# Two more weight tiles of each next matrix split ahead of a matrix boundary, in the idle activation region

## The reference

```python
h = rmsnorm(x, norm1_g[i]) * (1.0 + scale1) + shift1
y = diff_attention(h, ...)                 # i == 0: a_w_qkv, a_w_o
x = x + gate1 * y
h = rmsnorm(x, norm2_g[i]) * (1.0 + scale2) + shift2
x = x + gate2 * swiglu(h, f_w_in[i], f_w_out[i])
...
h2 = rms_norm(x, ffn_norm_g[layer])
up = h2 @ w_up[layer]
x = x + (jax.nn.gelu(conv(a)) * val) @ w_down[layer]
```

## Time and profile before

| | us |
|---|---|
| median of 3 runs (1039.02 to 1041.01) | 1040.88 |
| span of the profiled execution, first to last instruction | 1033.8 |
| PE busy | 986.3 |
| VectorE busy | 740.2 |
| ScalarE busy | 542.6 |

### The profile page before, as it was taken

The page is one execution under the profiler, slowest core; times in us unless marked ns, Lnnn a source line. Parts: engine busy times, 40 slices in busy tenths (PEclk is TensorE's granted clock), DMA queues, the critical chain, the costliest instruction groups (busy, mean ns, idle before and its releaser), DMA issues.

```text
span 1033.8 us, 13550 instructions
## 1 busy us (share of the span) xinstructions
PE 986.3 (95%) x5102; PEld 827.2 (80%) x5102; DVE 740.2 (72%) x1053; ACT 542.6 (52%) x875; POOL 68.4 (7%) x126
## 2 busy tenths in 40 slices
PE   2999799999999999999999999999999999999997
PEld 2887577888878787778888886888888779999986
DVE  5988888878877897887665447647753777777643
ACT  4466846544443485575444436575546474444442
POOL 2100222000000411010000002000000010000000
PEclk8999999999999999999999999999999999999999
DMA  9998167998889472449865553856444367656551
GB/s 339 371 371 285 39 204 230 344 321 295 273 304 359 162 250 101 143 127 321 263 203 186 183 184 108 269 160 205 134 142 143 119 190 218 187 177 189 184 184 41
DMA packets 126968, 219.89 MB, mean 213 GB/s; under 512 B 9235, under 2 KB 78088, under 8 KB 126904
## 3 DMA queue, kind: packets, MB, share of 16 engines
q1 hardware_dynamic: 125200, 215.52, 63.4%
q0 software_dynamic: 1088, 2.87, 0.8%
q10 hardware_dynamic: 616, 0.65, 0.2%
HBM read 217.96 MB, written 1.05 MB: 212 GB/s over the span
## 4 chain that ended last, share of the span: by engine, by line
PE 84%; DVE 8%; ACT 4%; issue 2%; DMA 1%; POOL 0%; SPq 0%; POOLq 0%; DVEq 0%; ACTq 0%
PE bank L1900 13%; PE bank L1902 13%; PE bank L1901 13%; PE bank L1913 5%; PE bank L1915 5%; PE bank L1914 5%; PE bank L2504 3%; PE bank L2505 3%; PE bank L2506 3%; DVE w_lo L1156 2%; PE bank L1961 2%; PE bank L1963 2%; PE bank L1962 2%; ACT w_hi L638 1%; DVE ada_acc L1186 1%
## 5 line engine op out<-in xcount | busy, mean ns | idle before, releaser
L1156 DVE TENSOR_TENSOR w_lo<-raw,w_hi 128x1024 fp32r<-128x1024 f32 x312 | 379.1, 1223 | 215.3 <-ACT w_hi L638 214.5
L638 ACT ACTIVATE w_hi<-raw 128x1024 fp32r<-128x1024 f32 x312 | 328.2, 1061 | 338.4 <-PE bank L1902 139.7
L1900 PE MATMUL bank<-w_hi,h_hi 128*128 128x512 f32 x608 | 244.3, 402 | 3.7 <-DVE w_lo L1156 3.7
L1902 PE MATMUL bank<-w_hi,h_lo 128*128 128x512 f32 x608 | 238.3, 392 | 0.0
L1901 PE MATMUL bank<-w_lo,h_hi 128*128 128x512 f32 x608 | 237.9, 391 | 0.0
L1900 PEld LDWEIGHTS bank<-w_hi,h_hi 128*128 128x128 f32 x608 | 114.8, 189 | 28.4 <-issue 6.1
L1902 PEld LDWEIGHTS bank<-w_hi,h_lo 128*128 128x128 f32 x608 | 114.7, 189 | 24.6
L1901 PEld LDWEIGHTS bank<-w_lo,h_hi 128*128 128x128 f32 x608 | 114.9, 189 | 23.6 <-issue 1.0
L2504 PE MATMUL bank<-h_hi,w_hi 128*128 128x256 f32 x320 | 90.8, 284 | 1.1 <-DVE conv_t L1828 1.1
L2505 PE MATMUL bank<-h_hi,w_lo 128*128 128x256 f32 x320 | 90.7, 283 | 0.0
L2506 PE MATMUL bank<-h_lo,w_hi 128*128 128x256 f32 x320 | 90.7, 283 | 0.0
(11 more groups left out here) (328 smaller groups left out, 1372.2 us busy)
## 6 DMA issues: line engine op xcount, KB each, us to landing
raw<-in_f_w_in SPq DMA_DIRECT2D x176, 256.0 KB
ada<-in_ada_w SPq DMA_DIRECT2D x86, 512.0 KB, 5.9
raw<-in_w_in SPq DMA_DIRECT2D x46, 512.0 KB
raw<-in_f_w_out SPq DMA_DIRECT2D x44, 512.0 KB
raw<-in_w_up SPq DMA_DIRECT2D x88, 256.0 KB
raw<-in_a_w_qkv SPq DMA_DIRECT2D x24, 512.0 KB
raw<-in_w_down SPq DMA_DIRECT2D x22, 512.0 KB
raw<-in_b_w_qkv SPq DMA_DIRECT2D x12, 512.0 KB
```

The lines of the kernel that those rows point to most:

```text
L638: nc.scalar.activation(w_hi[:, m % SPL], raw[:, m % RAW], ACT.Copy).then_inc(hi_done, 1)
L1156: ve.tensor_tensor(w_lo[:, m % SPL], raw[:, m % RAW], w_hi[:, m % SPL].bitcast(F32), ALU.subtract).then_inc(lo_done, 1)
L1900: mm(o, hi, w_hi[:, s, k], start=(u == 0 and k == 0), stop=False)
L1902: last = mm(o, lo, w_hi[:, s, k], start=False, stop=(u == 3 and k == 1))
```

## The change

Ten tiles, the third and the fourth of the five matrices named above, leave the ring of six slots. They are "guests": their rounded and remainder parts go to four buffers laid over `u_hi` and `u_lo`. A guest waits only for tile nxt - 5, the last ahead of the four of `last_tall`. The other tiles take the six slots in turn without them, so nxt + 4 now has the slot of nxt - 4, nxt + 5 that of nxt - 3, and nxt + 6 to nxt + 9 those freed before nxt + 2. PE reads each tile where it lies.

```diff
+
+OPENED = (IN_0, QKV_B, IN_1, IN_C, UP_C)
+GUESTS = {n + 2 + e: e for n in OPENED for e in range(2)}
+
+
+def ring_slots():
+
+    slot, freed_by, last, turn = {}, {}, {}, 0
+    for m in range(END):
+        if m in GUESTS:
+            freed_by[m] = m - 2 - GUESTS[m] - 5
+            continue
+        slot[m] = turn % SPL
+        if slot[m] in last:
+            freed_by[m] = last[slot[m]]
+        last[slot[m]] = m
+        turn += 1
+    return slot, freed_by
+
+
+SLOT, FREED_BY = ring_slots()
...
         u_lo = at_u("u_lo", [P, KF, S], KF * S, F32R)
+        guest_hi = [at_u(f"guest_hi{e}", [P, 2, CH], 1024 * e, F32R) for e in range(2)]
+        guest_lo = [at_u(f"guest_lo{e}", [P, 2, CH], first, F32R) for e, first in enumerate((2048, 5632))]
         qkT = at_u("qkT", [P, 16, S], 0)
...
+        def hi_of(m):
+            return guest_hi[GUESTS[m]][:] if m in GUESTS else w_hi[:, SLOT[m]]
+
+        def lo_of(m):
+            return guest_lo[GUESTS[m]][:] if m in GUESTS else w_lo[:, SLOT[m]]
```

The parts of `split`, the two `boundary` functions and their surroundings:

```diff
                 m = at(m, turn, LOOP)
                 act.wait_ge(raw_in[m % RAW], 32 * (m // RAW + 1))
-                if m >= SPL:
-                    act.wait_ge(mm_done, m - SPL + 1)
-                nc.scalar.activation(w_hi[:, m % SPL], raw[:, m % RAW], ACT.Copy).then_inc(hi_done, 1)
+                if m in FREED_BY:
+                    act.wait_ge(mm_done, FREED_BY[m] + 1)
+                nc.scalar.activation(hi_of(m), raw[:, m % RAW], ACT.Copy).then_inc(hi_done, 1)
...
             def boundary(r, o, nxt, gain, shift=None):
 
-                first = nxt - SKEW + SPL
                 for n in range(2):
                     part_square(r, 0, n)
+                if r == 0:
+                    split(nxt + 2)
                 part_scale(r, 0)
                 if shift is not None:
                     act.wait_ge(gain_ok, r + 3)
                 part_operand(o, 0, 0, gain, shift)
                 part_operand(o, 0, 1, gain, shift)
-                split(first)
-                part_square(r, 1, 0)
-                part_square(r, 1, 1)
+                if r == 0:
+                    split(nxt + 3)
+                    part_square(r, 1, 0)
                 part_operand(o, 0, 2, gain, shift)
                 part_operand(o, 0, 3, gain, shift)
-                split(first + 1)
+                if r:
+                    part_square(r, 1, 0)
+                part_square(r, 1, 1)
+                split(nxt + 4)
                 part_scale(r, 1)
-                for p in range(2):
+                for p in range(4):
                     part_operand(o, 1, p, gain, shift)
-                split(first + 2)
-                part_operand(o, 1, 2, gain, shift)
-                part_operand(o, 1, 3, gain, shift)
-                split(first + 3)
+                split(nxt + 5)
...
+                split(base + 4 * NCH_FF + KF + 2)
+                split(base + 4 * NCH_FF + KF + 3)
...
+            split(IN_1 + 2)
+            split(IN_1 + 3)
             boundary(2, 2, IN_1, gains, mod[:, 72:80])
...
+            split(UP_C + 2)
+            split(UP_C + 3)
             boundary(4, 5, UP_C, vecs[:, FFN_V:FFN_V + KD])
...
             def boundary(r, s, o, nxt, gain, shift=None, gated=None, before=None):
 
-                first = nxt - SKEW + SPL
                 if r == 3:
                     v_.wait_ge(late_in[1], 16)
                 part_residual(r, s, nxt, 0, 0, gated)
@@ -1305,19 +1339,17 @@
                 part_scale(r, 0)
                 part_residual(r, s, nxt, 1, 0, gated)
                 part_operand(o, 0, 0, gain, shift)
+                part_operand(o, 0, 1, gain, shift)
                 part_residual(r, s, nxt, 1, 1, gated)
-                part_operand(o, 0, 1, gain, shift)
-                low(first)
                 part_operand(o, 0, 2, gain, shift)
+                if r == 0:
+                    low(nxt + 3)
                 part_operand(o, 0, 3, gain, shift)
-                low(first + 1)
                 part_scale(r, 1)
-                for p in range(2):
+                low(nxt + 4)
+                for p in range(4):
                     part_operand(o, 1, p, gain, shift)
-                low(first + 2)
-                part_operand(o, 1, 2, gain, shift)
-                part_operand(o, 1, 3, gain, shift)
-                low(first + 3)
+                low(nxt + 5)
...
                 low(IN_0)
                 low(IN_0 + 1)
+                low(IN_0 + 2)
 
             boundary(0, 0, 0, IN_0, gains, mod[:, 24:32], gated=0, before=gains_2)
 
...
+                low(base + 4 * NCH_FF + KF + 2)
+                low(base + 4 * NCH_FF + KF + 3)
...
             low(WO_B + 3 + SPL)
+            low(IN_1 + 2)
+            low(IN_1 + 3)
...
+            low(UP_C + 2)
+            low(UP_C + 3)
             boundary(4, 5, 5, UP_C, vecs[:, FFN_V:FFN_V + KD])
...
-                s = m % SPL
+                whi, wlo = hi_of(m), lo_of(m)
                 for t in range(T):
                     if t == 1 and wait_1 is not None:
                         pe.wait_ge(*wait_1)
                     o = bank[2 * b + t][:]
                     for k in range(2):
                         hi, lo = (h[:, 2 * u + k, t * P:(t + 1) * P] for h in (h_hi, h_lo))
-                        mm(o, hi, w_hi[:, s, k], start=(u == 0 and k == 0), stop=False)
-                        mm(o, hi, w_lo[:, s, k], start=False, stop=False)
-                        last = mm(o, lo, w_hi[:, s, k], start=False, stop=(u == 3 and k == 1))
+                        mm(o, hi, whi[:, k], start=(u == 0 and k == 0), stop=False)
+                        mm(o, hi, wlo[:, k], start=False, stop=False)
+                        last = mm(o, lo, whi[:, k], start=False, stop=(u == 3 and k == 1))
```

More of the change, by code:

```diff
@@ L1912, in tall @@
                         hi, lo = (h[:, k, t * P:(t + 1) * P] for h in (a_hi, a_lo))
-                        mm(o, hi, w_hi[:, s, n], start=first, stop=False)
-                        mm(o, hi, w_lo[:, s, n], start=False, stop=False)
-                        last = mm(o, lo, w_hi[:, s, n], start=False, stop=last_k)
+                        mm(o, hi, whi[:, n], start=first, stop=False)
+                        mm(o, hi, wlo[:, n], start=False, stop=False)
+                        last = mm(o, lo, whi[:, n], start=False, stop=last_k)
                 last.then_inc(mm_done, 1)
@@ L1924, in half_tall @@
                     hi, lo = (h[:, k, t * P:(t + 1) * P] for h in (a_hi, a_lo))
-                    mm(o, hi, w_hi[:, s, n], start=first, stop=False)
-                    mm(o, hi, w_lo[:, s, n], start=False, stop=False)
-                    last = mm(o, lo, w_hi[:, s, n], start=False, stop=False)
+                    mm(o, hi, whi[:, n], start=first, stop=False)
+                    mm(o, hi, wlo[:, n], start=False, stop=False)
+                    last = mm(o, lo, whi[:, n], start=False, stop=False)
                 if n == 0:
@@ L1939, in first_wide @@
                         pe.wait_ge(lo_done, m0 + u + 1)
[L1940 removed]
+                        whi, wlo = hi_of(m0 + u), lo_of(m0 + u)
                         for k in range(2):
                             hi, lo = (h[:, 2 * u + k, t * P:(t + 1) * P] for h in (h_hi, h_lo))
[L1943 to L1945 removed]
+                            mm(bank[t][:], hi, whi[:, k], start=(u == 0 and k == 0), stop=False)
+                            mm(bank[t][:], hi, wlo[:, k], start=False, stop=False)
+                            last = mm(bank[t][:], lo, whi[:, k], start=False, stop=(u == 3 and k == 1))
                         if t == T - 1:
@@ L1957, in part_tall @@
                     pe.wait_ge(lo_done, m0 + j + 1)
-                    s = (m0 + j) % SPL
+                    whi, wlo = hi_of(m0 + j), lo_of(m0 + j)
                     out_ = bank[base + banks[2 * n + t]][:]
                     hi, lo = (h[:, k0 + j, t * P:(t + 1) * P] for h in (a_hi, a_lo))
-                    mm(out_, hi, w_hi[:, s, n], start=(only and j == 0), stop=False)
-                    mm(out_, hi, w_lo[:, s, n], start=False, stop=False)
-                    last = mm(out_, lo, w_hi[:, s, n], start=False, stop=(last_k and j == count - 1))
+                    mm(out_, hi, whi[:, n], start=(only and j == 0), stop=False)
+                    mm(out_, hi, wlo[:, n], start=False, stop=False)
+                    last = mm(out_, lo, whi[:, n], start=False, stop=(last_k and j == count - 1))
                     if (t, n) == (T - 1, 1):
@@ L2438, in _ @@
                     pe.wait_ge(lo_done, IN_C + m + 1)
-                    s = (IN_C + m) % SPL
-                    whi, wlo = (w[:, s].rearrange("p a (b n) -> p (a b) n", b=2) for w in (w_hi, w_lo))
+                    whi, wlo = (w.rearrange("p a (b n) -> p (a b) n", b=2) for w in (hi_of(IN_C + m), lo_of(IN_C + m)))
                     for t in range(T):
@@ L2502, in up @@
                     for k in range(2):
```

(2 more changed lines are left out.)

13 lines of the change are left out of this document (4 added, 9 removed).

## The result

The changed kernel takes 1043.28 us in the median of 9 runs (1042.01 to 1046.81), the kernel before 1039.63 us in 9 runs beside it (1036.94 to 1041.01). The ratio is 1.0043, 95% interval 1.003 to 1.0056: slower, by 3.65 us.

A forecast was written before the change was run, and what follows sets the result against it. TensorE, busy 95% of a 1033.8 us span, bounds the kernel. IN_0 +0.3, QKV_B +1.0, IN_1 -0.3, IN_C -0.2, UP_C +2.4 sum to +3.2 us: 1040.9 becomes 1044.1, range 1039.5 to 1048.5.

The forecast's parts named there:

- The first chain: Residual to PE's transposes, tokens 0-127: early subtractions delay PE 2.3 us at QKV_B, 1.5 IN_1, 0.5 IN_C, 3.3 UP_C.
- the landing: At UP_C, transfers spread evenly: UP_C+2 lands about 829.6, UP_C+3 831.2; PE waits 3.3 us, 3.9 if latest.
- The second chain: Same for tokens 128-255: without the third tile's subtraction, 1.3 us back at QKV_B, 1.4 IN_1, 0.7 IN_C, nothing UP_C.
- rival (a): Granted clock falls behind the new waits at UP_C and QKV_B: one fall makes 1045.8, two 1047.5; chance 0.15.
- Later waits: After boundaries: act_u at IN_1 gives 0.4 us back; at UP_C av's 0.8 is absorbed, little of conv_t's 1.1.
- (b): Gain and loss cancel: first chain shorter once POOL is free, or UP_C's waits absorbed whole; 1041.5, chance 0.22.
- (c): Faster: both guest subtractions fit ahead of the first residual because DVE is not behind; -5.4, 1035.5, chance 0.12.
- (d): Early tiles change nothing because ACT's order delays them anyway; time as before, 1040.9, chance 0.03.
- The shared port: POOL's root waits out DVE's subtraction; without it, ready in 0.95 instead of 2.03 us; otherwise sum 2.2 higher.

The follow-up runs named there:

- before again: The kernel before once more, unchanged, against itself: ratio 1.0001, span 1038.0 us beside a time of 1039.78 us.
- mix: Against before: guests' subtractions behind first and second scale at QKV_B, IN_1, UP_C; changed kernel's way at IN_0, IN_C: 0.9949, repeated 0.9959.
- one ahead: Changed kernel, but at QKV_B and UP_C the fourth tile is split behind the first scale, subtracted behind the second; ratio to before 1.0001.
- changed again: The changed kernel once more, unchanged: ratio to before 1.0051, span 1040.9 us.
- splits ahead: Changed kernel, but VectorE subtracts the guests behind the first and second scale, except at IN_0; ratio to before 0.9994.
- guests behind: Changed kernel's slots, but no guest work ahead of the first residual at all five boundaries; subtractions behind first and second scale; ratio to before 0.9974.

## Why the forecast came out right, and where it did not

**The time.** 1044.1 was forecast, 1043.28 measured. The sum of +3.2 us stands against +3.65, and +2.9 to +3.5 between the spans of changed and of before again. Part of this agreement is luck. By the stretches (means of two profiles of each kernel) QKV_B and UP_C came out 1.4 and 0.9 above their terms, IN_0 1.0 below (within its chance), and IN_1 0.3 above and IN_C 0.3 below. Inside them, a fall of the clock that had been left out of the sum stands against gains that were left out too. The span of the first profile of before would have given +7.7; adding the sum to the median was right, but the 7.1 us between that span and the median are no property of the kernel: of the other thirteen profiled executions twelve have a span 1.7 to 2.1 us below their own time, and one 3.3.

**The first chain** (the mechanism of the forecast). Its steps are shown, by their waits and by taking them back. At QKV_B the wait went from 0.56 to 2.99, +2.43 for 2.3 forecast; at IN_1 it is 1.51 for 1.5; at IN_C it went from 0.78 to 1.35, +0.57 for 0.5; at UP_C it is 3.81 for 3.3. There the error is the landing: counted from the wait for `w_lo` (826.61 and 830.18) UP_C+2 came after 4.05 us and UP_C+3 after 5.44, where spreading the transfers evenly gave 3.0 and 4.6.

**The second chain** was over-sized at QKV_B and a little at IN_1. At IN_1 the root took 1.21 us from 451.57 on, not 0.95: it no longer waits out a tile's subtraction, but the operand pieces seem to hold it a little. The table of matmuls has 1.2 us back there, for 1.4. At QKV_B, where the stretches repeat, the gain by itself is 0.5 (mix, first wait unchanged) to 0.7 (one ahead, 0.99 more first wait and +0.29 in all), for 1.3. At IN_C it is 1.1 (0.57 paid, -0.50 in all), for 0.7.

At UP_C the forecast had nothing, since TensorE's list of waits shows none at the second transposes. That reading was wrong: the changed kernel makes up 0.8 to 0.9 us there (+5.62 to +4.75 and +5.38 to +4.55), and the mix, without a delay in the first chain, is 0.85 and 0.76 us ahead of before at the same matmul. In before the loss shows at the loading of the weights (PEld), which waited for VectorE three times:

```profile
837.93 0.19 PEld L1943 LDWEIGHTS bank<-w_hi,h_hi 128*128 128x128 f32 x1 [0.36 <-DVE h_lo L1292]
839.58 0.19 PEld L1943 LDWEIGHTS bank<-w_hi,h_hi 128*128 128x128 f32 x1 [0.43 <-DVE h_lo L1292]
841.80 0.42 PEld L1996 LDWEIGHTS bank<-ident,xn 128*128 128x128 f32 x4 [0.37 <-DVE xn L1267]
```

IN_0 was forecast at +0.3 and came out at -0.3 in eight of nine profiles with that code (the ninth, +1.28, has a longer clock fall), against 0 and +0.8 of before.

**The clock**, rival (a), is the step that failed: I gave it a chance of 0.15 and no term in the sum, and it fell behind both new waits in both profiles. The terms so are QKV_B +2.4 for +1.0, and UP_C +3.3 for +2.4 (means of two profiles each). Two falls did not bring 1047.5, because much of their price is made up again. Directly behind the first transposes each fall adds 1.4 to 1.7 us of lateness (+2.43 to +3.82 at QKV_B, +3.97 to +5.62 at UP_C, in changed again +2.39 to +3.80 and +3.91 to +5.38), near the 1.7 of the rival. Against one ahead, where the clock holds, 0.9 and 1.0 us of it are left when QKV_B's boundary is done, and 0.7 to 0.8 at the end of its stretch. At UP_C 0.3 and 0.2 are left behind the wait for `av`; what follows, the wait for `conv_t`, differs by more than that from run to run. The waits show where it goes: the one at the second transposes of QKV_B is 0.32 us instead of 0.51, and the 1.0 us for `av` at UP_C is absent. That the other engines catch up while TensorE runs at the lower level fits this; no run separates it from the longer wait.

**Later waits.** `act_u` at IN_1 went from 0.83 to 0.22, `av` was absorbed, `conv_t` was 1.47 and 0.54 where before had 1.11 and 1.25: as forecast, within chance. For `av` the reason given (TensorE comes later, so the wait is absorbed) does not hold by itself: in one ahead and in splits ahead TensorE comes 2.1 and 1.8 us later to UP_C's first transposes and still waits 1.01 and 0.99 us for `av`.

**The other rivals.** (b) is excluded by the interval. (c) had the right idea, that the second chains give time once the first is not delayed, and the wrong place. The mix, 5.3 and 4.7 us below before, comes near its 5.4, but that is in part luck: its terms were 1.3 for QKV_B, where the mix gains 0.5, and nothing for UP_C's second chain, where it gains 0.8. (d) is refuted by the rows: the early splits and subtractions did run ahead of the residual.

**The shared port.** The trace after bears the forecast out: at IN_0, with a third subtraction in a row, the root's second operation went from 0.58 to 1.40 us, and at IN_1, where the subtraction is gone, the first went from 1.23 to 0.56. One reading of the forecast was a little off. The root does not end when the subtraction does but a little later, 0.29 us at IN_1 (446.76 and 446.47) and 0.10 at IN_0 (156.21 and 156.11); 0.30 is what it takes alone. The Trainium skill, "SBUF — State Buffer", in the section on SBUF's two separate sides, has the shared port as an exclusive lock between a GpSimd operation that reads SBUF and a DVE operation with two SBUF inputs; these rows agree with it.

## What to carry to other kernels

Work that is made possible earlier must still be placed by slack, not by readiness: here the same ten buffers give 1.0043 or 0.995 by where their splits and subtractions stand in the lists of two engines. Look which chain is on the bounding engine's path at each boundary, and put the freed work behind its last link, unless the chain has slack: at IN_C the work ahead of the residual is the better place, -0.5 us against +0.15 in guests behind. Where the input is only then landing, an early wait stops a whole engine that works through its list in order.

Judge one profiled execution against the kernel's times before subtracting spans: two of the same kernel differed by 4.2 us, more than the effect. Where an engine's list is the same in both kernels, compare the starts of the same instruction. And a list of waits of the matmuls alone can miss time: look at the loading of weights too.
